# One residual feeding two norms: the first product of the second block on unnormalised rows in parts, and three smaller moves around it

## The reference, cut to what matters

```python
# end of first_block
h = h + swiglu_ffn(rms_norm(h, ffn_norm[layer]), ffn_w_in[layer], ffn_w_out[layer])
return rms_norm(h, final_norm)
# start of second_block, x is what first_block returned
mod = silu(c) @ w_ada[l] + b_ada[l]
sh1, sc1, g1, sh2, sc2, g2 = jnp.split(mod, 6, axis=-1)
h = rmsnorm(x, norm1_g[l]) * (1.0 + sc1[:, None, :]) + sh1[:, None, :]
proj = h @ w_in[l]          # q_m, k_m, v_m, q_d, k_d, v_d, gate_m, gate_d
...
x = x + g1[:, None, :] * (merged @ w_out[l])
h2 = rmsnorm(x, norm2_g[l]) * (1.0 + sc2[:, None, :]) + sh2[:, None, :]
x = x + g2[:, None, :] * hierarchical_moe(h2, ...)
```

## Time and profile before

| | us |
|---|---|
| median of three runs | 1309.88 |
| lowest, highest | 1301.74, 1312.49 |
| the profiled execution | 1310.17 |
| its span, first to last instruction | 1308.3 |
| PE busy in it | 1131.8 (87%) |
| DVE busy | 670.2 (51%) |
| ACT busy | 414.5 (32%) |
| mean granted TensorE clock | 0.948 |

### The profile page before, as it was taken

One profiled execution on the slowest core, in us unless ns is written; L12 is line 12 of the kernel. 1 busy time (PEld: TensorE's weight loads), 2 busy tenths in 40 slices (PEclk: granted clock), 3 DMA queues, 4 the chain that ended last, 5 costly groups with the idle time before them and its releaser, 6 DMA issues.

```text
span 1308.3 us, 23070 instructions
## 1 busy us (share of the span) xinstructions
PE 1131.8 (87%) x9324; PEld 921.2 (70%) x9325; DVE 670.2 (51%) x1040; ACT 414.5 (32%) x519; POOL 32.6 (2%) x71
## 2 busy tenths in 40 slices
PE   9999999999989999999899999778656667676666
PEld 8998999999868899999798899634223323332232
DVE  5799888886535565557256878542111122111113
ACT  3765333344474433335333673320000000000001
POOL 0000000000000000000100000000000000000000
PEclk9999999999999999999999999889888889888889
DMA  9577988855510965550945334689999999999996
GB/s 349 214 285 284 333 302 303 306 209 193 193 65 9 372 197 175 173 167 8 191 137 189 129 138 191 255 315 428 429 428 429 428 429 429 429 427 430 428 430 258
DMA packets 99400, 362.47 MB, mean 277 GB/s; under 512 B 4160, under 2 KB 51664, under 8 KB 84112
## 3 DMA queue, kind: packets, MB, share of 16 engines
q1 hardware_dynamic: 95216, 335.06, 67.2%
q0 software_dynamic: 3984, 26.50, 5.1%
q10 hardware_dynamic: 144, 0.10, 0.0%
HBM read 360.58 MB, written 1.06 MB: 276 GB/s over the span
## 4 chain that ended last, share of the span: by engine, by line
PE 59%; DMA 25%; DVE 9%; ACT 3%; issue 2%; SPq 1%; DVEq 0%; POOL 0%; POOLq 0%; ACTq 0%
DMA wbuf<-in_w_up 22%; PE ps L1843 16%; PE ps L1766 10%; PE ps L1729 8%; PE ps L2153 6%; PE ps L1750 3%; DVE parts L1077 3%; PE ps L2029 3%; PE ps L1775 2%; PE ps L1719 2%; PE ps L2203 2%; PE ps L2173 1%; DMA wbuf<-in_ffn_w_in 1%; PE ps L1926 1%; DMA wbuf<-in_lru_w_in 1%
## 5 line engine op out<-in xcount | busy, mean ns | idle before, releaser
L1843 PE MATMUL ps<-big_parts,parts 128*128 128x256 f32 x2112 | 259.6, 285 | 4.8 <-DVE parts L1077 3.7
L1843 PEld LDWEIGHTS ps<-big_parts,parts 128*128 128x128 f32 x2112 | 256.4, 191 | 6.0 <-DVE parts L1077 4.3
L2153 PE MATMUL ps<-wbuf,big 128*32 128x256 f32 x2176 | 166.9, 471 | 106.3 <-DMA wbuf<-in_w_up 103.0
L1077 DVE TENSOR_TENSOR parts<-wbuf,parts 128x2048 fp32r<-128x2048 f32 x90 | 204.4, 2287 | 89.4 <-ACT parts L822 45.2
L2153 PEld LDWEIGHTS ps<-wbuf,big 128*32 128x32 f32 x2176 | 92.9, 135 | 194.5 <-DMA wbuf<-in_w_up 84.4
L1639 DVE TENSOR_TENSOR big<-big,ps 128x128 f32<-128x128 f32 x33 | 9.5, 288 | 262.4 <-ACT big L1009 262.4
L1766 PE MATMUL ps<-big_parts,parts 128*128 128x256 f32 x1152 | 142.0, 283 | 1.7 <-DVE parts_f L1331 1.1
L1009 ACT ACTIVATE big<-ps 128x128 f32<-128x128 f32 x33 | 9.1, 277 | 421.9 <-PE ps L2153 421.9
L1766 PEld LDWEIGHTS ps<-big_parts,parts 128*128 128x128 f32 x1152 | 139.3, 189 | 2.1 <-issue 1.3
L1729 PE MATMUL ps<-parts_f,parts 128*128 128x256 f32 x720 | 103.0, 284 | 0.0
L1729 PEld LDWEIGHTS ps<-parts_f,parts 128*128 128x128 f32 x720 | 93.6, 192 | 0.1
(11 more groups left out here) (334 smaller groups left out, 1388.2 us busy)
## 6 DMA issues: line engine op xcount, KB each, us to landing
wbuf<-in_w_down SPq DMA_DIRECT2D x32, 2048.0 KB, 38.0
wbuf<-in_w_gate SPq DMA_DIRECT2D x31, 2048.0 KB, 32.7
wbuf<-in_w_up SPq DMA_DIRECT2D x31, 2048.0 KB, 37.2
wbuf<-in_ffn_w_in SPq DMA_DIRECT2D x44, 1024.0 KB, 12.0
wbuf<-in_w_ada POOLq DMA_DIRECT2D x24, 1024.0 KB, 8.4
wbuf<-in_ffn_w_out SPq DMA_DIRECT2D x22, 1024.0 KB, 5.1
wbuf<-in_w_in SPq DMA_DIRECT2D x10, 2048.0 KB, 8.0
wbuf<-in_attn_w_qkv SPq DMA_DIRECT2D x6, 2048.0 KB, 8.6
```

Of the source, the lines that this page charges most:

```text
L1077: nc.vector.tensor_tensor(lo, whole, hi.bitcast(F32), ALU.subtract).then_inc(done, 1)
L1843: ins = mm(ps[:, b, d * 256:(d + 1) * 256], w[pw][:, k, d * P:(d + 1) * P], h_part_of[px][:, k], start=(k == 0 and d == 0 and i == 0), sto ...
L2153: ins = mm(at, rows, gu_place[s][:, :, k, r * P:(r + 1) * P], start=(k == 0), stop=(k == KC - 1))
```

## The change

- Both norms are taken from one residual. With x the residual, f the final norm's gain and r4 its root, the mean square of what norm 5 sees is r4 squared times the mean of (x f) squared. So DVE adds the banks once (`add_and_lower`), ACT and DVE split x times the joint gain (`gain[:, 0]` now contains f) into `x_shift_part`, and `qm` runs on that in parts, not normalised. Two more columns carry the shift through the same product (258 columns instead of 256), and DVE and ACT apply root and shifted bias to the result afterwards (`qm_scaled`, `qm_kept`).
- Both sums of squares are taken by two products each, behind the first half of `qm`. DVE forms the mean for norm 5 and the joint root `root_45`, then the normalised rows `hT`, which ACT shifts into `x_part[0]` directly; DVE makes the low part from `hT` and the shift. `km` takes column groups as they come (`product_pair_rows`). `xT` is normalised behind the split rows.
- `qm` is split where `vm` was (last step of the second net); `vm` is split behind `qm`'s result. `qm`'s high part lies in storage that `load_gate_up(sp, 0, 0)` overwrites, so that load now follows `qd`'s, which waits for `qm`; the rotary table is issued first.
- The modulation's arithmetic and lambda's sums are done by DVE ahead of the second net. POOL's store of the modulation waits for the second net's last weights (`fo_loaded[0]`) and no longer for the end of that net.
- `add_and_lower` is used at the entry of both feed-forward nets; the first pair of squares is added ahead of the last bank there, and `split_u(0, 0)` stands behind the squares.
- `SUM_BANK` changes for norms 4 and 5; `qm0` and `qm1` are no longer tiles of the rotating four banks.

```diff
+                elif name == "qm":
+                    act.wait_ge(ffn_gu, 2 * FFN_STEPS)
...
             wait_used(sp, f"ffn1_{FFN_STEPS - 1}")
+            sp.dma_start(rope, a["rope"]).then_inc(rope_in, 16)
+            load_unit("qd")
             load_gate_up(sp, 0, 0)
-            sp.wait_ge(h_ready, 4 * KC)
-            sp.dma_start(rope, a["rope"]).then_inc(rope_in, 16)
-            for name in RING[RING.index("qd"):]:
+            for name in RING[RING.index("kd"):]:
                 load_unit(name)
...
             pool.wait_ge(mod_ready, 2)
+            pool.wait_ge(fo_loaded[0], 16 * ffn_loads(1, FFN_STEPS - 1))
...
-            norm_square(4)
+            act.wait_ge(mod_ready, 2)
+            nc.scalar.activation(x_shift_part[0][:, :, SEQ:], ada[:, 0:KC].unsqueeze(2).to_broadcast([P, KC, 2]), ACT.Copy).then_inc(fh_hi, 1)
+            gained_high(4, x_rows_part[0], lambda k: gain[:, 0, k:k + 1])
+            for k in range(KC):
+                ins = nc.scalar.activation(squares[5][:, k], xT[:, k], ACT.Square, scale=col(R_FIN1 + k))
+                if k % 2 == 1:
+                    ins.then_inc(sq_done, 1)
             norm_root(4)
-            norm_square(5)
-            norm_root(5)
-            norm_shift(5, 0)
-            act.wait_ge(h_ready, 5 * KC)
-            for b in range(4):
-                nc.scalar.activation(x_part[0][:, 2 * b:2 * b + 2], hT[:, 2 * b:2 * b + 2], ACT.Copy).then_inc(fh_hi, 1)
-            copy_pair("qm0", qm[:, 0:2])
-            copy_pair("qm1", qm[:, 2:4])
+            act.wait_ge(sum_done, 6)
+            act.wait_ge(mean_ready, 1)
+            link(nc.scalar.activation(root_5, mean_5, ACT.Ln, bias=eps_col))
+            nc.scalar.activation(root_5, root_5, ACT.Exp, scale=-0.5).then_inc(root_done, 1)
+            def qm_shifted(h):
+                act.wait_ge(qm_scaled, h + 1)
+                for m in range(2 * h, 2 * h + 2):
+                    nc.scalar.activation(qm[:, m], qm[:, m], ACT.Identity, bias=qm_bias[:, m:m + 1]).then_inc(qm_kept, 1)
+            for k in range(KC):
+                act.wait_ge(h_part, k + 1)
+                nc.scalar.activation(x_part[0][:, k], hT[:, k], ACT.Identity, bias=ada[:, k:k + 1]).then_inc(fh_hi, 1)
+            qm_shifted(0)
+            qm_shifted(1)
+            hi_unit("vm")
             copy_pair("km0", km[:, 0:2])
...
-            def add_squares(n):
+            def add_squares(n, banks=(1, 2, 3)):
...
-            def add_and_lower(last, ready, parts_of, gains, before):
+            def add_and_lower(add, n, parts_of, gains, before, early_squares):
                 for b in range(5):
+                    if b == 3 and early_squares:
+                        add_squares(n, (1,))
                     if b < 4:
-                        add_bank(last, b)
+                        add(b)
                     if b:
-                        dve.wait_ge(x_ready, ready + b)
+                        dve.wait_ge(x_ready, 4 * (n - 1) + b)
                         gained_low(parts_of, gains, before, b - 1)
+                add_squares(n, (2, 3) if early_squares else (1, 2, 3))
+            add_and_lower(add_biased, 1, h_part_of, ffn_gains(0), fh_before[0], True)
+            split_u(0, 0)
             dve.wait_ge(silu_c, 1)
-            split_u(0, 0)
-            for b in range(4):
-                add_biased(b)
-                dve.wait_ge(x_ready, b + 1)
-                scaled_low(0, b)
-            add_squares(1)
             ada_unit(0)
             ada_unit(1)
...
-                        lo_unit("vm" if layer else "q0")
+                        lo_unit("qm" if layer else "q0")
...
-            for b in range(4):
-                add_bank("wo1", b)
-                dve.wait_ge(x_ready, 4 * 2 + b + 1)
-                scaled_low(1, b)
-            add_squares(3)
-            dve.wait_ge(root_done, 4)
-            ffn(1)
-            add_residual(f"ffn1_{FFN_STEPS - 1}")
+            add_and_lower(lambda b: add_bank("wo1", b), 3, h_part_of, ffn_gains(1), fh_before[1], True)
...
+            link(nc.vector.tensor_tensor(gain[:, 0], gain[:, 0], cols[:, R_FIN1:R_FIN1 + KC], ALU.mult))
...
-            norm_scale(4, lambda k: col(R_FIN1 + k), x_ready)
...
-            norm_scale(5, lambda k: gain[:, 0, k:k + 1])
-            for b in range(4):
-                subtract(x_part[1][:, 2 * b:2 * b + 2], hT[:, 2 * b:2 * b + 2], x_part[0][:, 2 * b:2 * b + 2], fh_hi, FH_LRU + 3 * KC + b + 1, fh_lo)
+            dve.wait_ge(root_done, 4)
+            ffn(1)
+            subtract(x_shift_part[1][:, :, SEQ:], ada[:, 0:KC].unsqueeze(2).to_broadcast([P, KC, 2]), x_shift_part[0][:, :, SEQ:], fh_hi, FH_QM + 1, fh_lo)
+            add_and_lower(lambda b: add_bank(f"ffn1_{FFN_STEPS - 1}", b), 4, x_rows_part, lambda k: gain[:, 0, k:k + 1], FH_QM + 1, False)
+            add_squares(5)
+            dve.wait_ge(root_done, 5)
+            dve.wait_ge(sum_done, 6)
+            link(nc.vector.scalar_tensor_tensor(out=mean_5, in0=ps[:, SUM_BANK[5], 0:SEQ], scalar=1.0 / D, in1=rstd[:], op0=ALU.mult, op1=ALU.mult))
+            nc.vector.tensor_tensor(mean_5, mean_5, rstd[:], ALU.mult).then_inc(mean_ready, 1)
+            dve.wait_ge(root_done, 6)
+            link(nc.vector.tensor_tensor(root_45, root_5, rstd[:], ALU.mult))
+            def shifted_low(k):
+                dve.wait_ge(fh_hi, FH_MOD + k + 1)
+                nc.vector.scalar_tensor_tensor(out=x_part[1][:, k], in0=hT[:, k], scalar=ada[:, k:k + 1], in1=x_part[0][:, k].bitcast(F32),
+                                               op0=ALU.add, op1=ALU.subtract).then_inc(fh_lo, 1)
+            for k in range(KC):
+                nc.vector.scalar_tensor_tensor(out=hT[:, k], in0=xT[:, k], scalar=gain[:, 0, k:k + 1], in1=root_45, op0=ALU.mult, op1=ALU.mult).then_inc(h_part, 1)
+                if k:
+                    shifted_low(k - 1)
+            shifted_low(KC - 1)
+            for h in range(2):
+                dve.wait_ge(qm_done, h + 1)
+                nc.vector.tensor_copy(qm_bias[:, 2 * h:2 * h + 2].unsqueeze(2), ps[:, 4 + 2 * h:6 + 2 * h, SEQ:SEQ + 1])
+                nc.vector.tensor_tensor(qm[:, 2 * h:2 * h + 2], ps[:, 4 + 2 * h:6 + 2 * h, 0:SEQ], root_45.unsqueeze(1).to_broadcast([P, 2, SEQ]), ALU.mult).then_inc(qm_scaled, 1)
+            for k in range(KC):
+                ins = nc.vector.scalar_tensor_tensor(out=xT[:, k], in0=xT[:, k], scalar=col(R_FIN1 + k), in1=rstd[:], op0=ALU.mult, op1=ALU.mult)
+                if k % 2 == 1:
+                    ins.then_inc(x_ready, 1)
+            lo_unit("vm")
...
-            norm_sums(4)
-            norm_sums(5)
+            def qm_product(h):
+                w = unit_parts("qm")
+                for k in range(KC):
+                    if h == 0:
+                        pe.wait_ge(fh_lo, FH_QM + 1 + k + 1)
+                    for m in range(2 * h, 2 * h + 2):
+                        for i, (px, pw) in enumerate(PART_PAIRS):
+                            ins = mm(ps[:, 4 + m, 0:SEQ + 2], w[pw][:, k, m * P:(m + 1) * P], x_shift_part[px][:, k],
+                                     start=(k == 0 and i == 0), stop=(k == KC - 1 and i == 2))
+                ins.then_inc(qm_done, 1)
...
-            for h in range(2):
-                second_product("qm", h)
-            pe.wait_ge(fh_lo, FH_LRU + 3 * KC + 4)
-            second_product("km", 0)
+            wait_parts("qm")
+            qm_product(0)
+            for n in (4, 5):
+                sums_added(n).then_inc(sum_done, 1)
+            qm_product(1)
+            wait_parts("km")
+            product_pair_rows("km0", unit_parts("km"), 0, KC, x_part, FH_MOD)
             rotate("qm", qm, 0)
```

More of the change, by code:

```diff
@@ L77 @@
 WARM_UP = 20
-SUM_BANK = (7, 3, 5, 3, 0, 0, 0, 4)
+SUM_BANK = (7, 3, 5, 3, 3, 2, 0, 4)
 EXP_LN_TABLE = 6
@@ L192, in program @@
         square_0 = wbuf[:, 2 * MATRIX + KC * SEQ:3 * MATRIX].rearrange("p (k t) -> p k t", k=KC)
-        squares = [square_0, hT, hT, fm(WORK), hT, hT]
+        squares = [square_0, hT, hT, fm(WORK), hT, fm(WORK)]
         rg = wbuf[:, 2 * MATRIX:2 * MATRIX + KC * SEQ].rearrange("p (k t) -> p k t", k=KC)
@@ L223, in program @@
         c_row = flat(10272, D)
+        x_shift_part = [big_parts[:, WORK + 2048 + i * 2064:WORK + 2048 + (i + 1) * 2064].rearrange("p (k t) -> p k t", k=KC) for i in range(2)]
+        x_rows_part = [v[:, :, 0:SEQ] for v in x_shift_part]
+        mean_5, root_5, root_45 = (flat(TMP + 512 + SEQ * i, SEQ) for i in range(3))
+        qm_bias = small[:, 392:396]
         pbuf = [flat(TMP + 384 * i, 384) for i in range(2)]
@@ L362, in unit_parts @@
             k, lo = 4 if name[0] in "plow" else KC, (parts_0, parts_1, parts_2)[RING.index(name) % PLACES]
-            if name in SPLIT_2:
+            if name == "qm":
+                hi = parts[:, UNIT:2 * UNIT]
+            elif name in SPLIT_2:
                 at = HI_AT[SPLIT_2.index(name) % 2]
@@ L680, in norm_root @@
```

(26 more changed lines are left out.)

52 lines of the change are left out of this document (24 added, 28 removed).

## The result

| | us |
|---|---|
| changed kernel, median of 11 runs | 1296.5 (1294.38 to 1298.87) |
| kernel before, median of 11 runs beside it | 1306.94 (1301.74 to 1314.83) |
| ratio, 95% interval | 0.9917 (0.9897 to 0.9938) |
| the profiled execution after, its span | 1296.73, 1295.0 |
| PE, DVE, ACT busy in it | 1123.0, 685.3, 420.8 |

The medians, both taken side by side, differ by 10.4 us, 0.8%, and the interval of the ratio excludes 1. The profiled execution fell from 1310.17 to 1296.73 us, 13.4 us.

What follows compares the result with a forecast made beforehand. The experts' stage is bound by DMA and starts when earlier stages end, so time saved before 830 us comes off whole: 11.3 (joint norm) + 0.7 (first net's entry) = 12.0 us, from 1310.17 to 1298.2 us, range 1291 to 1306.

Steps and rivals of the forecast that it cites:

- Rival (d): At the experts' stream or a transfer, the time gained is waited off: 1309.5 us; chance 0.06.
- The joint norm: From the second net's end to `vm`: the new order makes `vm` start 11.3 us earlier.
- sequence copied from the stick attention's entry: Around `qm`'s first half: adds, splits and product timed as in that attention, 5.99 us for 48 matmuls.
- second wait: TensorE's gap before the second sum of squares, behind `qm`'s first half: about 1.2 us.
- what comes behind `km`: At `rotate` and `vm`: 0.2 us lost, then 0.2 to 0.3 us, because `qm`'s result and `vm`'s parts are late.
- 0.2 us lost: At `rotate`: `qm`'s result ready at 641.3, wanted when `km`'s first half ends at 641.1.
- The cover: `qm`'s second half and `km`'s start hide roots and normalised columns; the eighth column has 0.9 us to spare.
- The first net's entry: VectorE's adds follow the banks, with `split_u` behind the squares: 0.7 us gained.
- The store: POOL's modulation store moved ahead: no gain or loss, at most one unit's 7.9 us if uncovered.
- Rival (a): The clock falls inside `qm`, costing 2.9 us: 9.1 us gained, 1301.1 us; chance 0.10.
- Rival (c): `qm`'s matmuls of 258 columns are slower, at 0.44 us each adding 30.6 us: 1328.8 us; chance 0.03.
- rival (b): Larger gain: the second net's 2.9 us stall at 455 us falls otherwise or small waits vanish: 1294.8 us; chance 0.13.

Runs made afterwards that it cites:

- The fill: 20 spare matmuls ahead of TensorE's wait for `qd`'s parts, against the split-first kernel: 1293.38 us, ratio to the kernel before 0.9875.
- split-first kernel: Changed kernel with `split_u(0, 0)` put back ahead of the adds at the first net's entry: 1293.56 us, ratio to the kernel before 0.9873.
- filled kernel before: Kernel before with spare matmuls, results never read, put into three places in TensorE's order: 1310.51 us, ratio to the unfilled kernel before 1.0012.

## Why the prediction was right

**The bound.** What was gained ahead of the experts' stream arrived: 13.0 us at the last output projections, 13.3 at the end. Rival (d), that the gain doesn't arrive, is out.

**The joint norm: booked 11.3 us, measured 11.9.** To `km` it was forecast 12.0 and measured 27.48 - 15.54 = 11.9. The sequence copied from the stick attention's entry was right: 0.30 us to `qm`, 6.01 us for 48 matmuls. Behind it, two small errors cancel: the second wait was 0.93 us and not 1.2, and each sum of four records took 1.13 us and not 0.9 (a row of the first net's entry had the 1.13). The term that was mis-sized is what comes behind `km`, 0.7 us of loss that did not occur. The copies of the bias take 0.15 us and start 0.07 ahead of the scaling, VectorE begins to normalise `xT` at once, and the low half of `vm`'s weights ends at 639.87 + 4.49 = 644.36, 0.55 us ahead of `vm`. The step "0.2 us lost" at `rotate` was close all the same: with `km` 0.7 us earlier, `rotate` waits 0.36 us.

**The cover.** It was named as what the gain rests on, and taking it away cost 7.4 us in the median and 6.5 at `km`. The spare time behind it was forecast at 0.9 us and came to 1.3: the eighth column was ready at 635.45, and `km` reads it at 631.68 + 7 x 0.72 = 636.7.

**The first net's entry: booked 0.7 us, measured 1.6.** The direction was right, the size less than half. Two pieces made it. I charged each pair of operations its own 0.87 us, while in a row they follow each other every 0.79 (a bank's add at 97.35, the low rows at 98.14), so the split started at 103.36 and not at 104.0. And I took 0.2 us off for a wait of TensorE on this split; what TensorE waits for at 113.08 is the split after it, and VectorE hands its lead of 1.6 us to that one whole. What the forecast did not ask is whether the old place of the split was the better one. TensorE closes its banks from 93.4 to 99.2 us, so VectorE, ready at 93.6, has to wait between adds (0.95 us at 95.47), and the split fits there.

**The store: booked at nothing, rightly, with a wrong bound beside it.** "One unit's 7.9 us at most" if the cover were gone: without it, 17.4 us. The bound took the stores to cost no more than one more transfer of weights. In the run, SP needed 21.20 us to issue a single transfer beside them, and the one behind it was late as well. The share of 2.61 with falling throughput was the sign; it came again as 2.28 at 193 GB/s. The other queues held: ScalarE starts on `kd`'s weights at 658.09 us, behind a wait for TensorE and none for the load.

**The clock.** Rival (a) did not occur: 1.00 throughout `qm`, as the row with the 0.75 us gap had suggested. The advice that the prediction takes from the Trainium skill, "TensorE: Matmul & The Clock Gate", part 1, is against longer gaps than these, so it did not speak against this order. Rival (c) is out as well: in the chain, 48 matmuls of 258 columns take 5.75 us, exactly as `km`'s 48 of 256 behind them, 0.120 us each. The 6.01 us of the timeline are to be set against the 5.99 that it has for 256 columns.

**The sum.** The forecast of 1298.2 us started from the profiled 1310.17. In the medians the gain was 10.4 us, 1.6 less than the 12.0 forecast (from the ratio's interval, 8.1 to 13.5); that 1296.5 still lies below 1298.2 comes from the kernel before, which took 1306.94 in these runs, and is luck. Against the forecast 12.0 us of gain, the profiled spans differ by 13.3: 12.0 + 0.5 (the entry, as far as it is seen at 455 us) + 2.5 (from there to the second net's end) + 0.6 (the norm) - 2.3 (behind `vm`). The 2.5 are the gate product's 13.15 in place of 14.43 us, and a slightly faster pace of the whole net. The 2.3 are the two products of 7.5 us, 3.0 us together, less some tenths won back elsewhere. Neither is the change's doing in the way the forecast meant it: rival (b) had the first, and nothing had the second. That the forecast lies 1.5 us from the profiled execution is therefore partly that these two cancel, each larger than what is left.

## What to carry to other kernels

Before a root or any chain of small operations, look for a product that needs only what lies before it, scale its result afterwards, and check the cover at both ends: here it was worth about 7 us to have it, and the next 0.7 us of TensorE's idle time were worth nothing, because the other chain was as long. When an order is copied from one place to another, lay each engine's waits beside it: where VectorE waits for a bank, a piece of its later work may fit. Keep stores of single elements out of the time in which weights are loaded; here 12 KB of them cost 17.4 us.

## What was unexpected

- The fall of the clock behind TensorE's wait of 2.71 us near 780 us. It occurs in all nine profiles that have the joint norm and no fill at this place (three of the changed kernel, six of the edited ones), and in none of the three without the joint norm, though the kernel before waits 2.71 us at the same place and then takes 5.99 us. The fill speaks for the wait as a condition; why the kernel before escapes is open. The fall near 697 is less regular: five of the nine unfilled profiles with the joint norm have it, and neither of the two without the joint norm. Other falls do change between executions of one kernel: of the two profiles of the split-first kernel, one has a fall at 452 to 456 us and the other has none there and one at 366 to 370. The Trainium skill, "TensorE: Matmul & The Clock Gate", part 1, says that the chip's watch on TensorE's activity runs free of the kernel, so that the point at which the clock changes varies between runs. The falls that change from execution to execution agree with it; nine of nine and none of three look less like chance, and no run here decides it.
- Two paces of the second net. A down product of 48 matmuls takes 5.76 us in the kernel before and in one profile of the changed kernel, and 5.70 us in the first profile of the changed kernel and in most others, the filled kernel before among them: 120.0 against 118.7 ns a matmul, some 1.5 us over the net. It goes with the execution and not with the kernel; what sets it was not tried.
